# Five more pairs of products in seven multiplications per block, with ten more weight sums, 24 of all 60 formed in block 0

## The reference, cut to what matters

```python
h = rmsnorm(x, g_pre[l])
proj = h @ w_in[l]                      # 1024 -> 12*512 + 4*1024
v_n = layernorm(a_v, ln_v_g[l], ln_v_b[l])
out_a = gmlp_spatial(a_u, v_n, w_s[l], b_s[l]) * jax.nn.silu(a_z)
glu = b_a * jax.nn.sigmoid(b_b)         # 31 taps, layernorm, silu -> out_b
out_c = multiscale_pool(ext_c, start_pos, pool_w[l], pool_scale[l]) * jax.nn.silu(c_z)
out_d = d_b * causal_depthwise(ext_d, conv_d_w[l]) * jax.nn.silu(d_z)
gates = jax.nn.sigmoid(gate_logits + b_gate[l]).reshape(bsz, t, N_BRANCH, D_MODEL)
merged = sum(gates[:, :, i] * (out_i @ w_branch[l, i]))   # four terms
x = x + rmsnorm(merged @ w_out[l], g_post[l])
```

## Time and profile before

| | |
|---|---|
| median of three runs | 2374.4 us |
| the profiled execution | 2372.7 us, span 2370.9 us |
| TensorE busy | 2353.2 us (99%), 13240 matmuls |
| VectorE busy | 1563.9 us (66%) |
| GpSimd busy | 639.9 us (27%), all but a little in blocks 0 and 1 |
| ScalarE busy | 442.7 us (19%) |
| DMA | 686.62 MB, mean 290 GB/s |

### The profile page before, as it was taken

How to read it: one execution, slowest core, us unless ns; L and a number is a source line. 1 busy time by engine, 2 the same in 40 slices (tenths; PEclk the granted TensorE clock), 3 DMA queues, 4 the chain that set the end, 5 groups by cost and what they waited for, 6 DMA issues and landing times.

```text
span 2370.9 us, 34948 instructions
## 1 busy us (share of the span) xinstructions
PE 2353.2 (99%) x13240; PEld 2086.4 (88%) x13240; DVE 1563.9 (66%) x2349; ACT 442.7 (19%) x646; POOL 639.9 (27%) x423
## 2 busy tenths in 40 slices
PE   9999999999999999999999999999999999999998
PEld 7888888888888888788888899999899999999998
DVE  7886886854666578875276856776337786577643
ACT  5222222323112111121101100111110110010111
POOL 4534544455645646666200000000100000000000
PEclk9999999999999999999999999999999999999999
DMA  8877879788987988999764699999774458988884
GB/s 329 321 248 278 309 258 328 279 289 335 394 323 286 359 327 328 379 340 361 287 242 179 214 327 369 311 326 326 269 252 161 159 187 286 331 282 268 279 282 176
DMA packets 220673, 686.62 MB, mean 290 GB/s; under 512 B 18096, under 2 KB 19760, under 8 KB 186736
## 3 DMA queue, kind: packets, MB, share of 16 engines
q1 hardware_dynamic: 207920, 652.18, 76.9%
q10 hardware_dynamic: 12608, 32.49, 3.7%
HBM read 514.14 MB, written 170.46 MB: 289 GB/s over the span
## 4 chain that ended last, share of the span: by engine, by line
PE 92%; DVE 5%; DVEq 1%; DMA 1%; issue 1%; ACT 0%; POOL 0%; POOLq 0%; SPq 0%; ACTq 0%
PE acc L1925 50%; PE acc L2146 18%; PE side L2157 7%; PE side L2069 4%; PE side L2146 4%; PE acc L2306 3%; PE side L2306 3%; DMA w_pair<-split_main 1%; PE acc L2303 1%; PE side L2303 1%; PE side L2097 1%; PE side L2087 1%; DVE t_sum L1410 0%; PE acc L2336 0%; DVE cb L1197 0%
## 5 line engine op out<-in xcount | busy, mean ns | idle before, releaser
L1925 PE MATMUL acc<-h_hi,w_pair 128*128 128x512 f32 x2752 | 864.2, 390 | 3.5 <-DMA w_pair<-split_main 3.4
L1925 PEld LDWEIGHTS acc<-h_hi,w_pair 128*128 128x128 f32 x2752 | 516.7, 188 | 111.4 <-issue 3.8
L1925 PE MATMUL acc<-h_lo,w_pair 128*128 128x512 f32 x1376 | 535.3, 389 | 0.0
L1197 DVE SCALAR_TENSOR_TENSOR cb<-glu,col,cb 128x512 f32<-128x512 f32 x600 | 425.5, 775 | 18.5 <-issue 10.5
L643 POOL TENSOR_TENSOR w_pair<-w_raw,w_pair 128x1024 fp32r<-128x1024 f32 x118 | 268.4, 2286 | 272.6 <-ACT w_pair L776 257.5
L675 POOL TENSOR_TENSOR rstd<-msq,nhalf 128x5 f32<-128x5 f32 (+4 forms) x19 | 19.9, 1047 | 1125.5 <-DVE msq L1107 531.8
L1925 PEld LDWEIGHTS acc<-h_lo,w_pair 128*128 128x128 f32 x1376 | 258.4, 188 | 53.4
L2146 PE MATMUL acc<-t_hi,chunk 128*128 128x256 f32 (+1 forms) x1344 | 266.9, 287 | 1.3 <-DVE merged L1502 1.3
L2146 PEld LDWEIGHTS acc<-t_hi,chunk 128*128 128x128 f32 x1344 | 216.6, 189 | 1.9 <-DVE merged L1502 1.7
L2146 PE MATMUL acc<-h_hi,chunk 128*128 128x256 f32 (+1 forms) x1008 | 205.0, 289 | 2.4 <-issue 1.3
L2146 PE MATMUL acc<-t_lo,chunk 128*128 128x256 f32 (+1 forms) x672 | 193.1, 287 | 0.0
(11 more groups left out here) (327 smaller groups left out, 3409.2 us busy)
## 6 DMA issues: line engine op xcount, KB each, us to landing
w_pair<-split_main SPq DMA_DIRECT2D x118, 1024.0 KB, 6.3
chunk<-split_main SPq DMA_DIRECT2D x226, 512.0 KB, 5.6
chunk<-s_parts SPq DMA_DIRECT2D x200, 512.0 KB, 6.0
split_main<-w_pair SPq DMA_DIRECT2D x88, 1024.0 KB, 6.4
s_parts<-s_out SPq DMA_DIRECT2D x50, 1024.0 KB, 5.8
w_raw<-in_w_main SPq DMA_DIRECT2D x88, 512.0 KB, 4.6
chunk<-split_branch SPq DMA_DIRECT2D x62, 512.0 KB, 4.4
s_raw<-in_w_half SPq DMA_DIRECT2D x50, 512.0 KB, 6.6
```

The costliest lines, as they stand in the source:

```text
L1197: dve.scalar_tensor_tensor(dst, src, c1("conv_w", c * CK + t), dst, ALU.mult, ALU.add)
L1925: ins = pe.matmul(acc[:, s, b, 0:m], w_k[:, wt, wk], mv_[:, k, t0:t0 + m], start=(k == 0 and n == 0), stop=(k == nk - 1 and n == 2))
```

## The change

Section M and the first two gates' pair of G0 join the scheme of seven products in blocks 2 and 3: five more pairs each (`SEVEN` now starts with M, 4 pairs, and G0 has 4). That needs ten more halves of weight sums, 60 in all. The first 24 (`HALF0`) are now made in block 0, one for every four units, with one raw buffer and one sum buffer; the other 36 in block 1. The four sums of h are formed in the output projection of the block before, from the unsplit h (four operations), and their low parts there too, on VectorE. GpSimd's loops are written out. In blocks 2 and 3 one tap group (`conv_step`) each moves from C and M to later sections, and three stand inside `seven_d`.

```diff
-SEVEN = [("G0", 3), ("D", 8), ("G1", 4), ("G2", 4), ("Z", 2), ("G3", 4)]
+SEVEN = [("M", 4), ("G0", 4), ("D", 8), ("G1", 4), ("G2", 4), ("Z", 2), ("G3", 4)]
-SEVEN_AT = UNIT0["G0"] + 4
+SEVEN_AT = UNIT0["M"]
-HALF_LOAD = [h * 29 // 25 for h in range(NH)]
-HALF_CAST = [max(0, 2 * s - 1) for s in HALF_LOAD]
-HALF_STORE = [s + 2 for s in HALF_LOAD]
-HALF_POOL = [2 * s for s in HALF_LOAD]
+HALF0 = 24
+X_ROWS_AT = UNIT0["G2"] // 2 + 1
+SLOTS = [s for s in range(50) if not X_ROWS_AT <= s < X_ROWS_AT + 4]
+HALF_SLOT = [SLOTS[h * len(SLOTS) // (NH - HALF0)] for h in range(NH - HALF0)]
+HALF_LOAD = [16 + 4 * h for h in range(HALF0)] + [UPB + 2 * s for s in HALF_SLOT]
+HALF_STORE = [19 + 4 * h for h in range(HALF0)] + [UPB + 2 * s + 4 for s in HALF_SLOT]
+HALF_CAST = [10 + 4 * h for h in range(HALF0)] + [UPB + max(0, 2 * s - 1) for s in HALF_SLOT]
+HALF_SUM = [10 + 4 * h for h in range(HALF0)] + [UPB + 2 * s for s in HALF_SLOT]
+HALF_LOW = [11 + 4 * h for h in range(HALF0)] + [UPB + 2 * s for s in HALF_SLOT]
+RAW_OF = [0 if h < HALF0 else (h - HALF0) % 3 for h in range(NH)]
+SUM_OF = [0 if h < HALF0 else (h - HALF0) % 2 for h in range(NH)]
...
+        for u, (name, r) in enumerate(units):
+            m = unit_pieces(name, r)[0][1]
+            if half_unit(u):
+                raw_load(u, raw_branch_rows(m), WB)
+            else:
+                raw_load(u, raw_rows(m), DM)
...
+                    split_store(u - RING, split_rows(m), DM)
+            sum_moves(u)
...
+        def s_sums(h):
+
+            a11, a12, a21, a22 = (s_raw[RAW_OF[h]][:, c, :] for c in range(4))
+            s1, s2, s3, s4 = (s_sum[SUM_OF[h]][:, c, 1, :] for c in range(4))
+            pool.wait_ge(s_loaded[RAW_OF[h]], 16 * (RAW_OF[:h].count(RAW_OF[h]) + 1))
+            if SUM_OF[h] in SUM_OF[:h]:
+                pool.wait_ge(s_stored[SUM_OF[h]], 16 * SUM_OF[:h].count(SUM_OF[h]))
...
+        def s_low(h):
+
+            out = s_out[SUM_OF[h]]
             pool.wait_ge(s_hi_done, h + 1)
...
+            for r in range(count):
+                u = UNIT0[name] + r
+                tick(u)
...
+                sum_steps(u)
...
+        def t_sums(j):
+            b11, b12, b21, b22 = (h_x[:, c0:c0 + CT, t0:t0 + hw] for c0 in (0, CT) for t0 in (0, hw))
...
+            dve.tensor_tensor(t1, b12, b11, ALU.subtract).then_inc(t_summed, 1)
+            dve.tensor_tensor(t3, b12, b22, ALU.subtract).then_inc(t_summed, 1)
+            dve.drain()
+            dve.tensor_tensor(t2, b22, t1, ALU.subtract).then_inc(t_summed, 1)
+            dve.drain()
+            dve.tensor_tensor(t4, b21, t2, ALU.subtract).then_inc(t_summed, 1)
...
+            def seven_m(c):
+
+                p = PAIRS.index(("M", c))
+                pair_sums(p, lambda: m_side(c))
...
+                if i < 3:
+                    conv_step(j, 19 + i)
                 pair_sums(p + 1)
...
             if not last:
+                if is_seven(j + 1):
+                    for t, casts in ((3, 2), (1, 3), (2, 4), (4, 4)):
+                        t_low(j + 1, t, casts)
```

More of the change, by code:

```diff
@@ L428, in gate_unit, with sigs_of @@
         name, q = PAIRS[p]
-        return 2 * (q + (name == "G0")) + t
+        return 2 * q + t
+    def sigs_of(name, q):
+        return q % 2 if name == "D" else 1 if name == "M" else 2
     def sigs_before(j, p):
-        n = sum(q % 2 if name == "D" else 2 for name, q in PAIRS[:p])
-        return n + (j - SEVEN0) * sum(q % 2 if name == "D" else 2 for name, q in PAIRS)
+        n = sum(sigs_of(*pair) for pair in PAIRS[:p])
+        return n + (j - SEVEN0) * sum(sigs_of(*pair) for pair in PAIRS)
     def unrolled(eng, j, start, end, body):
@@ L557, in _ @@
                     sp.dma_start(dst, src).then_inc(const_loaded, 16)
[L558 to L562, removed]
-            sp.wait_ge(split_stored[r], 16 * (UPB // RING))
[L564 to L573, removed]
+        for u in range(UPB - RING, UPB):
+            split_store(u, split_rows(unit_pieces(*units[u])[0][1]), DM)
+        for r in range(RING):
+            sp.wait_ge(split_stored[r], 16 * (UPB // RING))
         def chunk_source(kind, m, c):
@@ L664, in s_half, with sum_steps @@
             pool.drain().then_inc(s_summed, 1)
+        def s_low(h):
+            out = s_out[SUM_OF[h]]
             pool.wait_ge(s_hi_done, h + 1)
-            pool.tensor_tensor(s_out[h % 2][:, :, 1, :], s_sum[h % 2][:, :, 1, :], f(s_out[h % 2])[:, :, 0, :],
+            pool.tensor_tensor(out[:, :, 1, :], s_sum[SUM_OF[h]][:, :, 1, :], f(out)[:, :, 0, :],
                                ALU.subtract).then_inc(s_lo_done, 1)
+        def sum_steps(step):
+            for h in range(NH):
+                if HALF_LOW[h] == step and h < HALF0:
+                    s_low(h)
+            for h in range(NH):
+                if HALF_SUM[h] == step:
+                    s_sums(h)
+                    if h >= HALF0:
+                        s_low(h)
         powers = [0]
@@ L942, in _ @@
                 c = r // 4 * 2 + r % 2
+                if last and r == 2:
+                    act.wait_ge(vn_ready, j + 1)
+                    act.dma_start(v_s, lnv_g_bc[0:DEC, :]).then_inc(v_stored, 16)
+                if last and r == 3:
+                    act.wait_ge(v_stored, 16)
                 if r % 4 < 2:
@@ L967, in _ @@
                 s_cast(j, u)
-                if last and r == 1:
-                    act.wait_ge(vn_ready, j + 1)
-                    act.dma_start(v_s, lnv_g_bc[0:DEC, :]).then_inc(v_stored, 16)
             def gates(name, qg):
@@ L1432, in _ @@
                 dve.drain().then_inc(side_free, 1)
+            for c in range(0 if is_seven(j) else CT):
+                u = ub + UNIT0["M"] + 2 * c
+                m_side(c)
                 ready_at(0, u // 2)
@@ L2113, in _ @@
                     m_job(r // 2 - 1)
-            m_job(3)
+            if not is_seven(j):
+                m_job(3)
             def gated(ph, start, end, job=None):
@@ L2238, in _ @@
             if is_seven(j):
-                gated(0, 0, 1)
                 seven_pairs()
```

375 lines of the change are left out of this document (166 added, 209 removed).

## The result

| | before | after |
|---|---|---|
| median | 2374.46 us (4 runs, 2374.11 to 2375.16) | 2554.74 us (4 runs, 2551.35 to 2555.29) |
| ratio | | 1.0756, 95% interval 1.0737 to 1.0775 |
| span of the profiled execution | 2370.9 us | 2553.5 us |

What follows compares the result with a forecast made beforehand. TensorE's own work was taken as the bound. From 2372.7 us, +159 (block 0), -13.9 (fewer products), -2.6 (section M's waits) and +1.7 (block 3 waits) gave 2517, stated as 2518 us; range 2440 to 2570.

Steps and rivals of the forecast that it cites:

- the chain: Block 0, every four units: load, sums, casts, low parts in sequence; 28.1 us between full units, 25.4 in G sections.
- +159 in block 0: Net loss from the 24 early halves making TensorE wait for GpSimd: 173 us, less 14 for faster sums.
- tile 12: Block 0 weight tile, first of a four-unit cycle numbered 12 to 16; its finished low part lets the half's load be issued.
- the short sums: GpSimd's four sums per block 0 half taken at 3.5 us, not 4.1: 0.6 us less in each of 24 cycles.
- X: Block 0, from the end of tile 12 to the half's landing: 11.8 us between full units, 10.0 in G sections.
- its own three transfers alone: Block 0 case where the half queues only behind tile 16's raw load and tile 12's store: landing after 8.0 us.
- TensorE's waits for line 640: Sign in block 0: 24 or fewer waits for GpSimd's low parts, each 4 to 9 us, together 140 to 180 us.
- the second branch of the rival: Block 0: the clock falls but recovers each cycle, inside TensorE's slack, costing nothing; the clock rival had 3%.
- The seven products: Blocks 2 and 3: five pairs replace ten full units in each block, saving 4.8 and 9.1 us, 13.9 in all.
- the D waits: Block 3: taps in `seven_d` delay the next pair's first sum; TensorE waits 0.6 us three times, +1.7 us.
- the wait that was left out: Block 1: 36 halves in place of 50 may end its one 3.4 us wait; not counted in the sum.
- the lead covers it: Rival: GpSimd's idle time and three-unit lead absorb block 0's new work if cycles stay within about 17 us; 2358 us, 3%.

Runs made afterwards that it cites:

- e2: Changed kernel with each block 0 half's load queued two units earlier, behind tile 10's low part: 2434.5 us, ratio 1.0253.
- e7: Changed kernel loading only the first half in block 0, the other 23 summed from the same buffer without a load: 2433.9 us, ratio 1.0250.
- e3: Changed kernel with ScalarE's cast of the block 0 sums one unit later, after its cast of tile 14: 2504.7 us, ratio 1.0548.
- e9: Changed kernel with e2's earlier load and each block 0 half's store one unit earlier, behind that of tile 14: 2411.4 us, ratio 1.0151.
- e4: Changed kernel with the edits of e9 and e3 together (load, store and cast moved): 2394.8 us, ratio 1.0085.
- e11: e4 with GpSimd's and ScalarE's operations for 23 of block 0's 24 halves on a sixteenth of their columns: 2357.0 us, ratio 0.9926.

## Why the prediction was right

**Right in its mechanism.** TensorE waited for line 640 of GpSimd, GpSimd for the half, the half for its place in the queue. e2 and e7 (the load), e3 (the cast) and e9 with e4 (the store) took the chain apart link by link.

**The mis-sized term: +159 in block 0, measured +198.5.** From the end of one tile 12 to that of the next, the nine cycles with full units took 28.2 us in the mean (27.5 forecast with the short sums), the fourteen in G sections 27.0 (24.8): 9 x 0.7 + 14 x 2.2 = 37 of the 39.5 us of the miss. The term that was too small is above all X in G sections: 11.7 us in the mean in place of 10.0, 24 us over fourteen cycles. Between full units it was 12.2 in place of 11.8. In the cycle shown the half was issued at 509.25, 1.65 us behind tile 12, where the timeline of before had suggested some 0.8: the issue of the store ahead of it took 1.20 us, not 0.43, and its own 1.57. It landed 10.7 us after its issue began. So the landings in the earlier trace rows held no queue as full as this one. One cycle shows the other case: at 648.8 us the half was issued 0.88 us behind tile 12, landed 7.1 us later, and X was 8.1 us, which is the prediction's 8.0 for its own three transfers alone. The sums went the other way: four took 3.3 us in the mean and mostly under 3.2, not 3.5, near the low end of the earlier trace rows. The casts with their hand-overs came as forecast, 2.2 to 2.3 us; the low parts of the sums and of tile 16 took 2.7 us each, where 2.4 and 2.5 were forecast.

**What was looked for.** GpSimd's first sum waited for the load in each of the 24 cycles, as forecast; in the cycle shown it landed 12.3 us after the group's first issue. But TensorE's waits for line 640 were 79 us in 13, not 140 to 180 in up to 24. Of the same chain, other waits carry other names: 40.6 us stand under ScalarE's zc lines, since ScalarE stood at the cast of the sums, and all behind it in its program stood with it:

```profile
523.25 1.06 ACT L778 ACTIVATE s_out<-s_sum 128x1024 fp32r<-128x1024 f32 x1 [14.81 <-POOLq L661]
```

All of TensorE's waits in block 0 together are 142 us, within what the prediction gave to line 640 alone. The other 57 us of the loss are matmuls at the slower clock inside the same slack. Whoever had counted line 640 alone would have found two fifths of the cost.

**The clock.** It fell to 0.50, that is 1.2 GHz, in the idle part of a cycle, stayed there for the first matmuls after it, and was back at the full 2.4 GHz for the rest: 0.81 on the average of the cycle shown. That is the second branch of the rival, and agrees with the page of the Trainium skill cited for it (TensorE: Matmul & The Clock Gate, The HAM clock gate). As the chain, not TensorE, set the cycle, the longer matmuls lay inside its waits and cost little; this is read from the timeline, and no run tried it alone. In e4, where TensorE no longer waits for GpSimd, its busy time is 15 us longer at a mean clock of 0.98, and that does lengthen the block.

**Blocks 1 to 3.** The seven products gave 13.9 us in blocks 2 and 3, net of the D waits; 14.8 was forecast. The D waits came to 2.2 us over three times, 1.7 forecast. No wait for chunks came in blocks 2 and 3. Block 1 gave 2.0, the wait that was left out.

**The rival on the other side, "the lead covers it".** Its sum was 2358 us, and it takes more than its condition. e4 fulfils the condition, since TensorE waits for no tile of GpSimd in its cycles, and stands at 2394.8. What it overlooked is GpSimd's effect on VectorE. The prediction had that effect in one sentence (GPSIMD Engine Reference, Key points, in the Trainium skill) with no price: it is 37 us for 24 halves, TensorE's lower clock between the small waits with it. e11, with that work nearly gone, is at 2357.0.

## What to carry to other kernels

Idle time of an engine is not a place for work until each input's position in the queue, each buffer's release, and the wait of every engine it passes through are read one by one; here each of the three links cost more than the whole gain. Shift such a chain by a unit or two before giving it up: three constants took 160 of 180 us. What GpSimd then still costs is paid by VectorE, whose instructions on SBUF tiles lengthen, and it shows only as small waits of TensorE for VectorE and a slower clock between them.

## What the runs showed of the hardware

- VectorE's `L1207` takes 746 ns with GpSimd idle and up to 2.9 us beside it. A cast of one SBUF tile lengthens as well, and as much: line 1190 of the kernel after, in block 2 with GpSimd nearly idle, and in block 0 beside it (ns, min/median/max). So it is not only instructions that read two tiles.

```profile
L1190 DVE CAST out_hi<-tmp x16: 426/426/429, 1449.6 to 1811.5; 128x512 fp32r<-128x512 f32 x16
```
```profile
L1190 DVE CAST out_hi<-tmp x16: 426/2406/2473, 115.5 to 646.1; 128x512 fp32r<-128x512 f32 x16
```

- Line 1507, which reads one operand from PSUM, did not lengthen: all 24 in block 0 of e4 (ns, min/median/max), with GpSimd busy 448 of 613 us.

```profile
L1507 DVE TENSOR_TENSOR tmp<-acc,sig x24: 690/692/694, 359.4 to 583.3; 128x512 f32<-128x512 f32 x24
```

- Issuing a DMA on SyncE's queue took 0.33 to 0.43 us where few were under way, and 1.20, 1.57 and 1.76 us for three in a row from 508.0 us on, the last of seven issued in some 6 us. The prediction's sum for X from the second half on had no term for the issues.
- Of 23 early halves, the full work and the narrow work differ by 104 us on GpSimd and by 96 us on VectorE: nearly one for one. It is no fixed price of GpSimd's busy time: e11 has 53 us more of it in block 0 than the kernel before, in instructions on 16 columns, and VectorE 2.7 us more; the changed kernel has 136 us more, over a longer block, and VectorE 53.
- GpSimd's side of it: line 655, a sum of 128x256, took 722 to 753 ns in the 24 of its 60 executions beside which VectorE was idle or nearly so, and up to 1285 ns in the others. That is what the prediction assumed when it priced the sums at the low end.
